# A chunked RWKV-7 scan: the backward inverse's transposed tile made on TensorE and copied by ScalarE instead of transposed by VectorE

## What is computed

```python
def _wkv7_step(S, inp):
    r_t, w_t, k_t, v_t, aa_t, bb_t = inp
    sa = jnp.einsum('zbhij,zbhj->zbhi', S, aa_t)
    S = S * w_t[..., None, :] + sa[..., :, None] * bb_t[..., None, :] + v_t[..., :, None] * k_t[..., None, :]
    y = jnp.einsum('zbhij,zbhj->zbhi', S, r_t)
    return S, y
...
    _, ys = lax.scan(_wkv7_step, S0, seq)
    y = jnp.sum(_flip_bwd(jnp.moveaxis(ys, 0, 2)), axis=0)
```

## Time and profile before

| | us |
|---|---|
| median of three executions | 4410.56 |
| lowest, highest | 4408.94, 4414.65 |
| the profiled execution | 4401.42 |
| its span, first to last instruction | 4399.4 |

### The profile page before, as it was taken

The page is one execution under the profiler, slowest core; times in us unless marked ns, Lnnn a source line. Parts: engine busy times, 40 slices in busy tenths (PEclk is TensorE's granted clock), DMA queues, the critical chain, the costliest instruction groups (busy, mean ns, idle before and its releaser), DMA issues. The chain is left out here.

```text
span 4399.4 us, 108173 instructions
## 1 busy us (share of the span) xinstructions
PE 4068.6 (92%) x47874; PEld 3460.0 (79%) x47874; DVE 2155.8 (49%) x3514; ACT 1387.9 (32%) x2961; POOL 1298.7 (30%) x902
## 2 busy tenths in 40 slices
PE   6999999999999997999968888888879999999999
PEld 5889668888888886887757777777757888888888
DVE  5661552452441543436767777777743353252441
ACT  3331672211110112234345555555532211111111
POOL 4111333111111112122156565666534211111111
PEclk8999999999999998999989999999979999999999
DMA  4232224113114112122232222222143212313213
GB/s 132 84 112 83 86 83 131 46 39 107 61 38 135 39 61 88 65 93 72 103 91 82 81 82 68 82 77 73 46 153 108 76 38 77 96 39 100 69 38 109
DMA packets 353473, 356.39 MB, mean 81 GB/s; under 512 B 18608, under 2 KB 324784, under 8 KB 350832
## 3 DMA queue, kind: packets, MB, share of 16 engines
q1 hardware_dynamic: 352144, 346.63, 24.8%
q10 hardware_dynamic: 864, 2.83, 0.2%
HBM read 247.16 MB, written 102.24 MB: 79 GB/s over the span
## 5 line engine op out<-in xcount | busy, mean ns | idle before, releaser
L449 POOL TENSOR_TENSOR mo_wlow<-mo_raw,mo_whigh 128x1024 fp32r<-128x1024 f32 (+1 forms) x148 | 350.5, 2368 | 1671.2 <-ACT mo_whigh L536 1671.2
L516 PE MATMUL f_ps<-fx_hh,mo_whigh 128*128 128x512 f32 (+1 forms) x2112 | 530.3, 359 | 0.0
L516 PE MATMUL f_ps<-fx_hl,mo_whigh 128*128 128x512 f32 (+1 forms) x2112 | 529.0, 358 | 0.0
L516 PE MATMUL f_ps<-fx_hh,mo_wlow 128*128 128x512 f32 (+1 forms) x2112 | 528.5, 358 | 0.0
L536 ACT ACTIVATE mo_whigh<-mo_raw 128x1024 fp32r<-128x1024 f32 (+1 forms) x148 | 152.3, 1029 | 863.9 <-PE f_ps L516 863.9
L516 PEld LDWEIGHTS f_ps<-fx_hl,mo_whigh 128*128 128x128 f32 x2112 | 349.3, 189 | 65.3
L516 PEld LDWEIGHTS f_ps<-fx_hh,mo_whigh 128*128 128x128 f32 x2112 | 349.6, 189 | 64.9
L516 PEld LDWEIGHTS f_ps<-fx_hh,mo_wlow 128*128 128x128 f32 x2112 | 348.8, 189 | 65.4
L601 DVE TENSOR_TENSOR f_xo<-f_ps,f_xo 128x512 f32<-128x512 f32 x168 | 90.8, 596 | 610.2 <-PE f_ps L516 578.1
L516 PE MATMUL f_ps<-mo_oh,mo_whigh 128*128 128x512 f32 (+1 forms) x1440 | 362.2, 360 | 9.8 <-PEq L56 9.8
L516 PE MATMUL f_ps<-mo_ol,mo_whigh 128*128 128x512 f32 (+1 forms) x1440 | 359.9, 358 | 0.0
(11 more groups left out here) (312 smaller groups left out, 8445.1 us busy)
## 6 DMA issues: line engine op xcount, KB each, us to landing
f_xo<-xres SPq DMA_DIRECT2D x64, 640.0 KB, 4.0
xres<-f_xo SPq DMA_DIRECT2D x48, 640.0 KB, 2.9
mo_raw<-in_ffn_w_gate SPq DMA_DIRECT2D x44, 512.0 KB, 3.7
mo_raw<-in_ffn_w_up SPq DMA_DIRECT2D x44, 512.0 KB, 3.8
sc_rk<-rkvl SPq DMA_DIRECT2D x80, 256.0 KB, 3.2
rkvl<-ri_ot SPq DMA_DIRECT2D x28, 640.0 KB, 3.0
mo_raw<-in_ffn_w_down SPq DMA_DIRECT2D x32, 448.0 KB, 4.2
qkn<-qkv_qk SPq DMA_DIRECT2D x16, 640.0 KB, 3.9
```

What stands on the lines that cost most here:

```text
L449: nc.gpsimd.tensor_tensor(wlow[:, m % 2, 0:kt], raw[:, 0:kt], whigh[:, m % 2, 0:kt].bitcast(F32), ALU.subtract).then_inc(cut_lo, 1)
L516: last = nc.tensor.matmul(ps[:, m % 2, n, 0:count], w[:, m % 2, k], x[:, k, t0:t0 + count], start=(k == 0 and w is whigh and x is xh), sto ...
```

## The change

After the last interleaved product of each odd step TensorE makes eight more products, `level_r`: the backward `tf` against the identity, into `t_ps[1]`, the half bank that `level_t` of the next step overwrites. ScalarE's `p_copy` for z = 1 first copies that half bank to `rf` and then `p_ps[1]` to `pt`, and signals once after both. VectorE's ten backward transposes into `rf` of each group are gone, with the signals `d_start` and `d_r[1]`.

```diff
+                def level_r(s, h, G):
+                    rows = halves[h]
+                    return nc.tensor.matmul(t_ps[1][side(h, 1), s * C:(s + 1) * C], tf[rows, G % 2, 1, s], ident[rows, rows], start=True, stop=True)
+
                 def level_t_waits(G, z, k):
                     pe.wait_ge(a_pt[z], 5 * G + k + 1)
-                    if k:
+                    if k and z == 0:
                         pe.wait_ge(d_r[z], 4 * G + k)
...
+                    if does_p and zp == 1:
+                        for s in range(U):
+                            for h in range(2):
+                                last_p = level_r(s, h, G)
                     if does_p:
                         last_p.then_inc(pe_p[zp], 1)
...
+                    if z == 1:
+                        if k == 0 and G >= 3:
+                            act.wait_ge(pe_u, 4 * G - 8)
+                        nc.scalar.activation(rf[:, G % 3, 1].rearrange("p s n -> p (s n)"), t_ps[1], ACT.Copy)
                     nc.scalar.activation(dst, src, ACT.Copy).then_inc(a_pt[z], 1)
...
                 def turn_t(G, z):
-                    if z == 0:
-                        return nc.vector.transpose(flat(rf[:, G % 3, z]), flat(tf[:, G % 2, z]))
-                    for h, rows in enumerate(halves):
-                        last = nc.vector.transpose(flat(rf[side(h, z), G % 3, z]), flat(tf[rows, G % 2, z]))
-                    return last
+                    return nc.vector.transpose(flat(rf[:, G % 3, z]), flat(tf[:, G % 2, z]))
...
-                    nc.vector.transpose(flat(tf[:, G % 2, z]), flat(r0[:])).then_inc(d_start, 1)
-                    dve.wait_ge(d_start, G + 1)
-                    if G >= 3:
-                        dve.wait_ge(pe_u, 4 * G - 8)
-                    turn_t(G, z).then_inc(d_first[z], 1)
+                    nc.vector.transpose(flat(tf[:, G % 2, z]), flat(r0[:])).then_inc(d_first[z], 1)
...
                         nc.vector.tensor_tensor(half, src, half, ALU.add).then_inc(d_t[z], 1)
-                        dve.wait_ge(d_t[z], 5 * G + k + 1)
-                        turn_t(G, z).then_inc(d_r[z], 1)
+                        if z == 0:
+                            dve.wait_ge(d_t[z], 5 * G + k + 1)
+                            turn_t(G, z).then_inc(d_r[z], 1)
...
                     if z == 1 and G >= 1:
-                        pool.wait_ge(d_start, G)
+                        pool.wait_ge(d_first[1], G)
```

More of the change, by code:

```diff
@@ L1624, in rwkv_scan @@
         a_pt, a_turn = ph.sems("a_pt", Z), ph.sems("a_turn", Z)
-        d_start, d_cum, d_tb, d_rec, d_bonus, d_two, d_st, a_y = (
-            ph.sem(x) for x in ("d_start", "d_cum", "d_tb", "d_rec", "d_bonus", "d_two", "d_st", "a_y"))
+        d_cum, d_tb, d_rec, d_bonus, d_two, d_st, a_y = (
+            ph.sem(x) for x in ("d_cum", "d_tb", "d_rec", "d_bonus", "d_two", "d_st", "a_y"))
         d_bm, d_gram, d_first, d_t, d_r = (ph.sems(x, Z) for x in ("d_bm", "d_gram", "d_first", "d_t", "d_r"))
```

## The result

The changed kernel takes 4486.18 us (median of four, 4479.72 to 4494.32) against 4411.97 us for the kernel before in the same comparison: a ratio of 1.0166, 95% interval 1.0153 to 1.0180. That is 74 us, 1.8 us for each of the 40 groups. The forecast was 4497, in 4455 to 4535.

What follows compares the result with a forecast made beforehand. TensorE was taken as bound by instruction delivery in about half of the scan. 2.36 - 0.3 + 0.1 = 2.16 us a group, 86 us over 40 groups, gave 4497 us, range 4455 to 4535.

Steps and rivals of the forecast that it cites:

- What bounds the scan: TensorE is bound by instruction delivery in about half of the scan, by its own work and the state chain elsewhere.
- starved block: About 256 TensorE instructions in the scan, ending in a stop for the next block; forecast at 3.77 us.
- The added products, 2.36 us: TensorE: 40 products, 160 instructions, 0.625 of a block a group; between 2.15 and 2.54 us, taken as 2.36.
- the two prices of a block: TensorE in the scan: 3.77 us for a block ending in a stop, 4.07 us for the mean of all blocks.
- VectorE's relief, 0.3 us: Ten transposes off VectorE let the state come earlier, mainly at step 4: 0.3 us a group gained, between 0 and 0.56.
- ScalarE's copies, 0.1 us: Five more PSUM copies a group on ScalarE, 0.38 us each, tightest at step 4: 0.1 us a group, bound 1.9.
- The sum, 2.16 us: Net cost for each of 40 groups in the scan: 24.1 to 26.3 us a group, 86 us in all.
- The main branch: The forecast itself, instruction delivery setting the cost in the scan: 4475 to 4530 us, 72%.
- A: Added products run in TensorE's idle time, VectorE decides: up to 0.56 us a group gained, -22 us, 4388; 4%.
- B: Half hidden: products fill TensorE's waits, state comes earlier, both in full; 1.6 us a group or less, 4450 to 4475; 12%.
- C: ScalarE's second copy delays chain or backward t: 4.4 us a group, 4588, at all five places; 4543 at two; 10%.
- The signs named in the profile: Scan: packets up a tenth at 3.9 to 4.1 us, groups 26 to 26.6 us, VectorE 176 us less, ScalarE 76 more.

Runs made afterwards that it cites:

- p products wide: Kernel before, with the eight p products of a level made as two of 256 columns, 240 instructions a group less: 4355.60 us, ratio 0.9872.
- change, p products wide: Changed kernel, with the eight p products of a level made as two of 256 columns: 4389.61 us, ratio 0.9940.
- change, added products wide: Changed kernel, with the eight added products of an odd step made as two of 256 columns, identity stationary: 4432.44 us, ratio 1.0049.
- products alone: Kernel before plus the 40 added products a group, read by nobody; VectorE keeps its transposes, ScalarE gets no copy: 4480.39 us, ratio 1.0156.
- products alone, four quarters: Kernel before plus 40 added products a group, read by nobody, half sent to the forward bank to use all four array quarters: 4483.90 us, ratio 1.0174.
- products twice: Kernel before plus the added products twice over, 80 a group, 320 instructions, read by nobody: 4589.72 us, ratio 1.0384.

## Why the prediction was right, step by step

The main runs in one table, by the instructions added to TensorE for each group; the last column has TensorE's stops for "issue" over the packets of queue 8 in the 850 us, the share of blocks that end in a stop:

| run | instructions a group | ratio | us a group | stops / packets |
|---|---|---|---|---|
| p products wide | -240 | 0.9872 | -1.41 | 46 / 187 |
| change, p products wide | -80 | 0.9940 | -0.66 | 70 / 200 |
| before | 0 | 1 | 0 | 110 / 209 |
| change, added products wide | +40 | 1.0049 | +0.54 | 105 / 206 |
| products alone | +160 | 1.0156 | +1.72 | 129 / 214 |
| products alone, four quarters | +160 | 1.0174 | +1.92 | 131 / 214 |
| the change | +160 | 1.0166 | +1.83 | 119 / 212 |
| products twice | +320 | 1.0384 | +4.23 | 127 / 212 |

**What bounds the scan.** Right, and "about half" as well: 110 of 209 blocks. Neither the columns nor the time on TensorE by itself accounts for the costs; the number of instructions does in the main. The price of one is not constant: between -240 and 0 it is 1.41 us / 240 = 5.9 ns, between 0 and +160 1.72 / 160 = 10.8 ns, between +160 and +320 2.51 / 160 = 15.7 ns (14.1 to 17.3). The last is that of a mean block, 4.01 us / 256 = 15.7 ns; a starved block's 3.87 / 256 = 15.1 lies inside its interval. The share of blocks that end in a stop explains the first rise (46 of 187, 110 of 209, 129 of 214), but not the second: with the products twice it is 127 of 212, no larger. There the time on TensorE may have its part.

**The added products, 2.36 us.** The mechanism was right, the size too high: measured 1.72 alone. I had called the two prices of a block the bounds from both sides, 3.77 and 4.07 us, and put the lower end at the time on TensorE, 2.15. But just before, the prediction had said that only about half of the scan waits for instructions; in the other half the starved price doesn't hold. The average price at this density is 1.72 / 0.625 = 2.8 us for a block. The bound of 2.15 from below was not one, for two reasons. It came from step 0, where the next line waits for the eight products; at the odd steps the chain's next product starts while they still run, and they lengthen the five steps by 1.48 us together. And part even of that fills time in which TensorE would have waited: in the kernel with wide p products the whole change costs 0.75 us a group. That 1.72 lies above 1.48 fits the stops, which grew from 110 to 129 though fewer groups lie in the window.

**VectorE's relief, 0.3 us.** Measured 0.2 for eight of the ten transposes alone (0.1 to 0.3 by its interval). In the change itself it can't be told from nothing (0.08 us, -0.1 to +0.3). The forecast took the relief and the added products as independent, and they are not: the products alone bring TensorE's wait on the state from 16.4 to 2.4 us in the 850, and what is no longer waited for can't be gained again.

**ScalarE's copies, 0.1 us.** Measured nothing alone, between -0.15 and +0.04 us a group. In the change they may cost more: the run with the transposes put back has the products, the copies and the later signals and stands at 1.91 us a group, 0.19 over the products alone, with an interval from 0 to 0.4. TensorE's wait for `x_copy`, 4.3 us with the products alone, is 7.1 there and 7.6 in the change.

**The sum, 2.16 us.** Measured 1.83. The parts measured alone are 1.72 - 0.21 - 0.05 = 1.46; the whole has 0.37 us over them. If the four intervals are independent, that difference is uncertain by 0.26, so it is hardly noise alone; the two paragraphs above show where parts interact, about 0.1 for the relief and 0.2 for the copies, neither clear of noise by itself. The main branch, 4475 to 4530, was met with some luck: the term of the products was 0.64 us too high, and the parts as measured alone would give 4412 + 58 = 4470, below it. The mechanism and the direction were no luck.

**The rivals.** A (stops that cost nothing) is out: cost rises with instructions at every density tried. B (1.6 us) lies nearer to the measured 1.83 than the forecast's 2.16 does, nearer than its 12% said, and half of its mechanism is there: the products do fill waits. The other half, the relief in full, is not. C is out: TensorE's waits that name ScalarE are 11.5 us in the 850, 0.36 us a group, under the 0.5 that would have spoken for it. The signs named in the profile were there: 26.3 us a group, 4.01 us a packet, issue 121 us against 115, VectorE 180 us less, sixteen records of L1784 that start over 0.42 to 0.44 us, and no starved block cheaper than 3.6 us on average (3.87). ScalarE's 76 us more were 47.

## What to carry to other kernels

Where TensorE's idle time names nothing and its stops stand a fixed number of instructions apart, count instructions before columns: a float32 product of 64x64 is four of them, and forty such products cost 1.7 us of a group's 24. Then look whether the stops end at a fixed distance from instruction packets. The price of an instruction is not always that of a starved block; it was a good third of it where a quarter of the blocks end in a stop, and all of it where 60% do and TensorE has more work besides. Taking instructions out gained less than putting them in cost. And moving work off an engine that nobody waits for gains only what is waited for, here 0.2 us for eight transposes of 0.44, and nothing measurable once the other side of the change had made TensorE late. Before a shorter run of an instruction is used to tell two causes apart, measure in its trace, at like places, that it is shorter.

## What was not expected of the hardware

A matmul of 16 columns with its weight load took nearly as long in a row as one of 64 columns: sixteen records on two quarters of the array started over 0.39 us against 0.42 (first start to last start, medians of the steps without a stop). On four quarters sixteen records of the full width started over 0.35 us at the median, in some places over 0.22. Yet a step on four quarters was not much shorter, since the chain's next product could no longer start beside them.

In eight runs looked at (before, the change, wide, products alone, twice, four quarters, and the two with p products wide) the stops end at a median of 1.38 to 1.41 us after an instruction packet has ended, and each block that begins and ends with a stop holds the start of just one packet.
